# Two pairs of norms merged, tiles split at other points of a norm, and the first mixer's last part reordered, in a two-block float32 kernel

## What is computed

```python
def first_block(x, ...):
    for l in range(2):
        x = x + 0.5 * swiglu_ffn(rmsnorm(x, ffn1_norm[l]), ffn1_w_up[l], ffn1_w_down[l])
        x = x + mixer(rmsnorm(x, mix_norm[l]), w_in[l], ...)
        x = x + 0.5 * swiglu_ffn(rmsnorm(x, ffn2_norm[l]), ffn2_w_up[l], ffn2_w_down[l])
        x = rmsnorm(x, final_norm[l])

def mixer(h, ...):                      # of the first block
    z = h @ w_in + b_in                 # q, k, v, glu_in, gates
    y_attn = dilated_attention(q, k, v) @ w_attn_proj
    u = depthwise_conv31(a * sigmoid(g)) + conv_b
    u = layer_norm(u) * ln_g + ln_b
    y_conv = silu(u) @ w_conv_proj + b_conv_proj
    return (g_attn * y_attn + g_conv * y_conv) @ w_out

def second_block(x, c, ...):
    for i in range(2):
        mod = silu(c) @ mod_w[i] + mod_b[i]          # sh_m, sc_m, g_m, sh_f, sc_f, g_f
        h = rms_norm(x, norm_mix_pre[i]) * (1 + sc_m) + sh_m
        y = mixer_ab(h) if i == 0 else mixer_c(h)
        x = x + (1 + g_m) * rms_norm(y, norm_mix_post[i])
        h = rms_norm(x, norm_ffn_pre[i]) * (1 + sc_f) + sh_f
        y = conv_ffn(h)
        x = x + (1 + g_f) * rms_norm(y, norm_ffn_post[i])
```

## Time and profile before

| | |
|---|---|
| median of 3 runs | 2442.98 us (2442.26 to 2448.7) |
| the profiled execution | 2443.44 us |
| its span, first to last instruction | 2441.6 us |
| TensorE matmul, weight load | 2298.9 us (94%), 2238.6 (92%) |
| VectorE, ScalarE, GpSimd | 1727.7 (71%), 1192.4 (49%), 98.2 (4%) |
| granted TensorE clock, mean | 0.964 of full speed |

### The profile page before, as it was taken

The page is one execution under the profiler, slowest core; times in us unless marked ns, Lnnn a source line. Parts: engine busy times, 40 slices in busy tenths (PEclk is TensorE's granted clock), DMA queues, the critical chain, the costliest instruction groups (busy, mean ns, idle before and its releaser), DMA issues.

```text
span 2441.6 us, 45856 instructions
## 1 busy us (share of the span) xinstructions
PE 2298.9 (94%) x18202; PEld 2238.6 (92%) x18202; DVE 1727.7 (71%) x2811; ACT 1192.4 (49%) x1752; POOL 98.2 (4%) x196
## 2 busy tenths in 40 slices
PE   7999999989998999999998999899898999798997
PEld 6999999989998999999988999789887999797997
DVE  6667899767667766899866766586445766666766
ACT  4444444554444444454454544445454565444564
POOL 0000020000000000021000000000000000000000
PEclk8999999999999999999999999997799999998999
DMA  7775555235775777465324677343112455353552
GB/s 282 235 239 193 178 174 168 79 130 187 238 236 183 255 234 235 160 185 169 130 87 147 233 241 238 109 154 104 52 62 78 142 184 183 110 173 112 181 180 94
DMA packets 113503, 412.26 MB, mean 169 GB/s; under 512 B 13792, under 2 KB 13920, under 8 KB 112992
## 3 DMA queue, kind: packets, MB, share of 16 engines
q1 hardware_dynamic: 96192, 352.26, 42.8%
q0 software_dynamic: 16896, 56.64, 7.5%
q10 hardware_dynamic: 288, 1.57, 0.2%
HBM read 403.07 MB, written 1.05 MB: 166 GB/s over the span
## 4 chain that ended last, share of the span: by engine, by line
PE 88%; DVE 8%; ACT 3%; issue 1%; DMA 0%; DVEq 0%; ACTq 0%; SPq 0%
PE bank L503 86%; DVE w_lo L1370 2%; PE bank L643 1%; DVE arena L1533 1%; ACT w_hi L981 1%; DVE rinv L1404 1%; DVE work L1407 1%; DVE work L1439 1%; DVE h_lo L1398 0%; ACT rinv L1002 0%; ACT work L1123 0%; DVE rinv L1436 0%; ACT arena L1262 0%; ACT work L1000 0%; DMA tabs<-shape_tables 0%
## 5 line engine op out<-in xcount | busy, mean ns | idle before, releaser
L503 PE MATMUL bank<-h_hi,w_hi 128*128 128x256 f32 x3968 | 1151.2, 291 | 62.9 <-ACT h_hi L1008 27.9
L503 PE MATMUL bank<-h_hi,w_lo 128*128 128x256 f32 x3968 | 1135.1, 287 | 0.0
L503 PE MATMUL bank<-h_lo,w_hi 128*128 128x256 f32 x3968 | 1102.8, 284 | 0.0
L1370 DVE TENSOR_TENSOR w_lo<-w_raw,w_hi 128x1024 fp32r<-128x1024 f32 x663 | 808.6, 1222 | 373.5 <-ACT w_hi L981 367.1
L981 ACT ACTIVATE w_hi<-w_raw 128x1024 fp32r<-128x1024 f32 x663 | 699.8, 1057 | 638.7 <-PE bank L503 632.9
L503 PEld LDWEIGHTS bank<-h_hi,w_hi 128*128 128x128 f32 x3968 | 777.1, 196 | 80.9 <-issue 54.1
L503 PEld LDWEIGHTS bank<-h_hi,w_lo 128*128 128x128 f32 x3968 | 777.1, 196 | 0.0
L503 PEld LDWEIGHTS bank<-h_lo,w_hi 128*128 128x128 f32 x3968 | 755.3, 193 | 0.4 <-issue 0.2
L503 PE MATMUL bank<-hid_hi,w_hi 128*128 128x256 f32 (+1 forms) x1104 | 314.0, 284 | 9.4 <-ACT arena L1188 2.9
L503 PE MATMUL bank<-hid_lo,w_hi 128*128 128x256 f32 (+1 forms) x1104 | 312.2, 283 | 0.0
L503 PE MATMUL bank<-hid_hi,w_lo 128*128 128x256 f32 (+1 forms) x1104 | 311.9, 283 | 0.0
(11 more groups left out here) (217 smaller groups left out, 1887.3 us busy)
## 6 DMA issues: line engine op xcount, KB each, us to landing
w_raw<-weights SPq DMA_DIRECT2D x663, 512.0 KB, 3.4
mod_w_buf<-mod_w POOLq DMA_DIRECT2D x96, 512.0 KB, 4.8
mod_w_buf<-arena POOLq DMA_DIRECT2D x96, 64.0 KB, 3.7
tabs<-shape_tables SPq DMA_DIRECT2D x1, 1682.0 KB, 14.4
work<-v_bias ACTq DMA_DIRECT2D x2, 768.0 KB, 4.4
x<-x_fm SPq DMA_DIRECT2D x1, 1024.0 KB, 4.8
out_fm<-x SPq DMA_DIRECT2D x1, 1024.0 KB, 3.9
vecs<-vectors SPq DMA_DIRECT2D x1, 712.0 KB, 7.4
```

What stands on the lines that cost most here:

```text
L503: ins = pe.matmul(o, lhs, rhs, start=start, stop=stop, skip_group_check=share)
L1370: v.tensor_tensor(w_lo[:, n % SPLIT, :], w_raw[:, n % RAW, :], w_hi[:, n % SPLIT, :].bitcast(F32), ALU.subtract).then_inc(lo_ready[n % SPL ...
```

## The change

- **Merged pairs of norms.** `norm_pair` takes one root for two norms. With final gain g and second gain G, x g G / sqrt(mean(x^2 (g^2 + eps)) + eps^2) equals the two norms in a row. The weighted mean uses a column `pair_mean` as its stationary operand, the gains are `pair_gain`. A second mean (into bank 3) gives the root for x itself, which is renewed later: in the turns 3 to 5 of layer 1's first FFN, and for the second block in `recurrent_nsa_mixer`, from where ScalarE copies it back to x (`x_back`). The reordering of tokens is done by VectorE as it scales, in two instructions for each tile (`in_order`). The last `mod_cols` of each of the two layers goes behind the first pair of columns that follows.
- **Splits.** Tile t+2 is split by ScalarE directly behind the root of a norm, and by VectorE behind its low halves. At the end of an FFN the last split of VectorE goes behind the sums into x, and its last mod tile to turn 2. At the start three tiles are split ahead of the root.
- **`normed_pair`** takes each high tile for both columns before the next tile.
- **The first mixer's last part.** The mean of `conv` comes directly behind the units (bank 0), the variance behind the turned attention output (bank 1). Attention and the first four `gmix` tiles have operands of their own (`four_hi`, `four_lo`), so silu and its splits go in plain order beside the attention projection. `gmix` is split pair by pair, and the first `w_out` pair (`late_pair`) takes the first four tiles for both of its columns first.
- **Room.** `root_buf` moves to `mod_sum`, `vsw` to `mod_room`.

```diff
+        spare = sb("spare_operands", 4, SEQ, dt=F32R)
+        four_hi, four_lo = (hid_hi, spare[:, 0:2]), (hid_lo, spare[:, 2:4])
...
             def normed_pair(b):
-                for c, n in enumerate(tiles):
-                    for kt in range(KT):
-                        if c == 0:
-                            pe.wait_ge(h_high, w.next(h_high))
+                for kt in range(KT):
+                    pe.wait_ge(h_high, w.next(h_high))
+                    for c, n in enumerate(tiles):
                         mm(half(b, c), w_hi[:, n, at], h_hi[:, kt, :], ...)
                         mm(half(b, c), w_lo[:, n, at], h_hi[:, kt, :], ...)
...
+            def mean_pair(l):
+                for kt in range(KT):
+                    pe.wait_ge(sq_ready, w.next(sq_ready))
+                    mm(half(6, 0), pair_mean[:, l, kt:kt + 1].broadcast_to([P, P]), work[:, kt, :], ...)
+                for kt in range(KT):
+                    mm(half(3, 0), tab("mean_all"), work[:, kt, :], kt == 0, kt == KT - 1, square_used)
...
             (TensorE, first mixer, behind the units)
+                pe.wait_ge(conv_ready, w.next(conv_ready))
+                (8 matmuls: mean of conv into bank 0)
                 column_pair()
                 pe.wait_ge(ytm_ready, w.next(ytm_ready))
                 (8 turns)
+                (8 matmuls behind csq_ready: variance into bank 1)
                 column_pair()
-                (mean of conv into bank 6)
                 pe.wait_ge(ya_ready, w.next(ya_ready))
                 (4 attention pairs)
-                    (variance behind the second)
-                column_pair(csplit, order=list(range(GT, KT)) + list(range(GT)))
-                for i in range(1, KT // 2):
-                    column_pair(order=list(range(GT, KT)) + list(range(GT)))
                 for i in range(KT // 2):
-                    column_pair(gmix_ready if i == 0 else None, res_pair)
+                    column_pair(csplit if i == 0 else None)
+                hi, lo = four_in_spare(normed_hi, normed_lo)
+                late_pair(pair_bank(res_pair), gmix_ready, GT, hi, lo)
+                for i in range(1, KT // 2):
+                    column_pair(None, res_pair, hi=hi, lo=lo)
...
             (ScalarE)
+            def norm_pair(shift, o):
+                (squares of x into work)
+                act.wait_ge(stat_full, w.next(stat_full))
+                act_f(rinv[:, :], half(6, 0), ACT.Sqrt, bias=tab("eps_sq")).then_inc(root_ready, 1)
+                high_parts(state["tile"] + 2)
+                (h_hi for each scaled tile)
+                act.wait_ge(h_ready, w.last(h_ready))
+                act.wait_ge(square_used, w.next(square_used, KT))
+                act_f(o, half(3, 0), ACT.Sqrt, bias=tab("eps")).then_inc(root_ready, 1)
...
             def recurrent_nsa_mixer():
                 (two zk copies)
+                act.wait_ge(renewed, w.next(renewed, KT))
+                for k in range(0, KT, 4):
+                    ins = act_f(x[:, k:k + 4, :], work[:, k:k + 4, :], ACT.Copy)
+                ins.then_inc(x_back, 1)
...
             (VectorE, ffn_steps)
                     for j in range(FT):
                         hidden(j % 2)
-                        low_parts(min(t0 + 3 * j + 3, t0 + 3 * FT + 1))
-                        mod_tiles(2 if j < 2 else 1)
-                        low_parts(min(t0 + 3 * j + 5, t0 + 3 * FT + 1))
+                        if fresh and j == 0:
+                            mod_vector()
+                        low_parts(t0 + 3 * j + 3)
+                        if j < FT - 1:
+                            mod_tiles(2 if j < 3 else 1)
+                        low_parts(min(t0 + 3 * j + 5, t0 + 3 * FT))
+                        if fresh and j == 3:
+                            new_root(work[:, 0, :])
+                        if fresh and j in (4, 5):
+                            renew(range((j - 4) * KT // 2, (j - 3) * KT // 2))
                 (sums into x)
+                low_parts(t0 + 3 * FT + 1)
...
             (VectorE, recurrent_nsa_mixer)
-                skip_pairs(2)
+                skip_pairs(1)
+                mod_vector()
+                new_root(gate_a[:, 0, :])
+                for kt in range(KT):
+                    if kt == KT // 2:
+                        skip_pairs(1)
+                    in_order(kt, vec("final_norm", DEPTH - 1, 0, KT), gate_a[:, 0, :], renewed)
...
             (VectorE, first mixer's last part, new order)
+                (w_lo) (reciprocal, y_tm) (wait cmean_full: centring in two halves) next_pair
+                (wait yt_full: four_lo of the attention, ya_ready)
+                (wait croot: reciprocal, 8 scalings) next_pair, low_parts
+                for i in range(KT // 2):
+                    b, free = next_pair(1, wait=False)
+                    (low halves of silu tiles 2i, 2i + 1: csplit)
+                    dve.wait_ge(pair_full, w.last(pair_full))
+                    (gmix = attention pair * gates)
+                for i in range(KT // 2):
+                    (gmix += conv pair * gates)
+                    if i:
+                        gmix_low(i - 1)
+                gmix_low(KT // 2 - 1)
```

294 lines of the change are left out of this document (185 added, 109 removed).

## The result

The changed kernel takes 2403.6 us (median of 4 runs, 2399.0 to 2407.67) beside 2444.41 for the kernel before on the same chip: ratio 0.983, 95% interval 0.9807 to 0.9853. So it is faster, by 40.8 us (1.7%) and not by 47.7. A second set of four runs of the same kernel, on another chip, gave 2401.67. Both medians lie in the range of 2384 to 2414. Of the forecast's own stretch (2389 to 2402) the first lies just outside and the second just inside.

What follows compares the result with a forecast made beforehand. TensorE, busy 94% of the span, was taken as the bound, so only its idle or low-clock time could be won. Terms 4.8 + 5.4 + 9.2 + 22.6 + 1.2 + 3.5 + 1.0 = 47.7 off 2443.0 gave 2395.3 us, range 2384 to 2414.

Steps and rivals of the forecast that it cites:

- x sums ahead of the mean: FFN ends: mean starts right behind the last down product, 0.95 us earlier at each of five, 4.8 us gained.
- First pair: End of layer 0, first block: one root for two norms gains 7.4 us, mod columns cost 2.0, net 5.4.
- Second pair: Norms into the second block: gain 13.75 us, less 2.0 for mod columns and 2.5 for new waits, net 9.2.
- rival (a): Merged pairs: clock stays high in and behind them, two new stalls don't appear, 2388 us; chance 0.13.
- The mixer's last part: Behind the units, two layers: 12.1 us lost each, less a new 0.8 wait, so 11.3 per layer, 22.6 gained.
- Start: Kernel start: three tiles copied ahead of the root bring the first product sooner, 3.5 us gained, bounds 2 and 6.
- The w_lo wait of the earlier trace: Behind a mixer norm: splitting behind the root removes TensorE's wait for a low half, 0.6 us at each of two.
- The order's 1.0: First column pair behind some eight norms: new `normed_pair` order saves 0 to 0.3 us each, 1 us in all.
- The clock: Merged pairs: one stretch at the lower clock, costing about 1.7 us, stays in each; no gain counted.
- (b): Mixer's last part and second means: waits move instead of going, second means run at the lower clock, 2408 us; chance 0.20.
- (c): Mixer's last part: ring of three split tiles becomes a serial chain, every tile late, slower, 2453 us at 1.2 each; chance 0.02.
- a lower clock in the tail: Mixer's last part: sign of a wrong forecast, lower clock where none is now ahead of its long waits; no size given.

Runs made afterwards that it cites:

- with fill and the old order: Changed kernel plus unread matmuls in TensorE's waits, three added places included, with the earlier order of the first column pair behind a norm: 2385.71 us, ratio 0.9739.
- The kernel with fill: Changed kernel plus 78 matmuls that nobody reads, in TensorE's waits behind the means: 2386.06 us, ratio 0.974.

## Why the prediction was right, and where it was off

**x sums ahead of the mean.** Right in mechanism and size: 1.06 to 1.13 us a place against 0.95, within the bound of 1.1 or close to it. The medians don't show it, because in this kernel longer low stretches stand behind the mixer norms, which other kernels with the same early mean don't all have.

**First pair.** The first product came at root + 3.38, as taken. Measured 8.9 with the sums against 6.35. The term that was too careful is the clock: the pair behind takes 6.09 us instead of the 7.75 of before. The mod columns cost 1.83, for 2.0. The renewal on DVE showed as no wait of PE in turns 3 to 6.

**Second pair.** 11.4 with the sums against 10.15. The halves take 4.29 us for 16 (0.27 each, forecast 4.8 in all), the pair 7.38 (7.9). Both forecast waits are there, but PE loses only 1.0 of the 2.5, since 3.4 us of low clock (from 1525.4) slow PE's next pair by 1.7 meanwhile, and the late tile is wanted later. So the clock stays up through this pair and drops behind it: of rival (a)'s 2 x 1.7 only the first pair's 1.7 came.

**The mixer's last part.** The step that failed is a term of the sum: 11.3 per layer, with 8.3 measured. The four waits went as said and the new one came as said (0.64). But I took 12.1 lost us from the stretch that begins at 482.76, counted the new order at full clock there, and looked at no clock in front of it. The low stretch at the units' end costs 3.3 us in the changed kernel (1.1 in the last units, 2.2 in the mean). What brings it isn't the reordering: the kernel with the old last part has it too, and so does the one with a later mean. In the kernel before, the same sparse units ended 3 us later in the execution (20 in layer 1) and ran at 2.4 GHz, and its low stretch lay behind its 3.63 us wait instead (6.8 us from 520.6, and from 1285.2 in layer 1). So the change took one low stretch away with its wait and got one in another place. One later kernel, with fill and the old order, has none at layer 0's units either: 77.7 us from the last unit matmul to the last `w_out` product instead of 80.1. Against the 89.4 of before that is 11.7, so the 11.3 of the sum was right for a clock that stays up. All the other changed kernels have a low stretch there, of 3.4 or 6.8 us. What decides it was not settled.

**The rest.** Start 3.8 for 3.5. The w_lo wait of the earlier trace rows is gone, and hardly anything came of it: the clock behind the mixer norm took 6.8 us at the lower level instead of some 3.4. The order's 1.0 was too little: with the clock kept it saves 0.36 to 0.78 at each of nine norms, 5.4 in all.

**The sum.** That 44.4 us came out near 47.7 is in part luck. The start and the pairs brought 4.1 us more than their terms and the last part and the rest 7.4 less.

**The clock.** The forecast that a low stretch stays in each merged pair was wrong at the first, and the place where they cost was not foreseen. The reading of the earlier trace rows was off too: 0.57 over 4 us means 3.4 us at the lower level and not half of them; the 1.7 us that it costs is right. Nor did the change leave much less low clock in all: 175.4 us in the trace of before, 160.5 and 181.0 in the changed kernel's two. The Trainium skill ("TensorE: Matmul & The Clock Gate", Part 1) says that the gate follows how busy PE has been of late. By that rule the stretches at the merged pairs should go. The trace agrees at the first (1.00 from 761.00 to 774.10), and at the second for the pair of columns itself:

```profile
1515.90:1523.00 7.10, 7.05 (x46) 6.11 (x47) 7.10 (x21) 4.21 (x9) 0.00 (x0) 1.00 0.00 0
```

The kernel with fill agrees too: the stretches from 221.5, 566.3, 969.0, 1313.8 and 1525.4 are gone.

**The rivals.** (a) was true for the clock at the first pair, by 1.7, and not at the second. (b), waits that move, fell: the sum of waits in the tail is 0.6 us per layer. (c) fell as well: no wait for a weight tile in the last part but that 0.64. The time is above 2400, as the prediction said it would be if the tail's waits stayed, but the waits went. What came is another of its signs of being wrong, "a lower clock in the tail", which it had named and put no price on.

## What to carry to other kernels

Read the granted clock in front of the stretch that you cost, not only in it and behind it: a stretch counted at full pace that begins with PE's sparsest work can cost a third of the gain. Where a chain of small steps on other engines can't be shortened, unread matmuls in the wait kept PE at 2.4 GHz, which was worth 16 us here on one chip, beside some 41 for the whole change. They cost nothing as long as they end before what PE waits for: 14 of them, 6.3 us, held a mean by some 4.0. When single terms of 1 us are to be judged, compare equal products in two traces and fill the waits first; the medians of this kernel scatter by more.

## What the runs showed of the hardware

- The same instructions at the same place in the program ran at either level of the clock, depending on the kernel: the last 16 matmuls of the units in 1.99 us in the kernel before and 3.08 in the changed one.
- Behind the same norm, with the same idle time before it, the low stretch was 6.8 us in the changed kernel and 3.4 in four others, and the 48 products of the pair took 8.40 us or 7.31 to 7.41. The difference is as large as the 1.1 us that the step in front of the norm saves.
- The same wait of 3.6 us in the old last part was followed by 10.2 us of low clock in layer 0 and by 3.4 in layer 1 of one trace, and by 6.8 in both layers of the kernel before.
- One kernel's runs spread over 14.9 us (2391.34 to 2406.23) with mean clocks of 0.963 to 0.971. The kernels without unread matmuls spread over 1.8 to 16.1 us, those with them over 2.5 to 6.4.
